# One mLSTM layer in one stage: attention of heads and memory placed between the weight steps of 25 blocks

## What is computed

```python
h = rmsnorm(x, norm_g)
qk, v, o, z, i_pre, f_pre, mq, mz = split_cols(
    h @ w_in, [2 * M_WIDTH, M_WIDTH, M_WIDTH, M_WIDTH, M_HEADS, M_HEADS, MEM_WIDTH, MEM_WIDTH])
qk = jax.nn.silu(causal_conv(qk, conv_w, conv_b))
q, k = split_cols(qk, [M_WIDTH, M_WIDTH])
ht = mlstm_chunkwise(q, k, v, i_pre + ig_b, f_pre + fg_b)      # 4 heads of 256
ht = rmsnorm(ht, h_g)
y_m = jax.nn.sigmoid(o) * ht * jax.nn.silu(z)
y_mem = memory_attention(mq, mz, mk, mv, mq_gain)              # 4 heads of 128, 256 memory slots
return x + jnp.concatenate([y_m, y_mem], axis=-1) @ w_out
```

## Time and profile before

| | |
|---|---|
| median of three runs | 2470.48 us |
| profiled execution | 2471.05 us |
| its span, first to last instruction | 2468.8 us |
| TensorE matmuls, busy | 2256.1 us (91%) |
| VectorE, busy | 1781.2 us (72%) |
| ScalarE, busy | 1412.3 us (57%) |
| mean granted clock of TensorE | 0.968 |

### The profile page before, as it was taken

The page is one execution under the profiler, slowest core; times in us unless marked ns, Lnnn a source line. Parts: engine busy times, 40 slices in busy tenths (PEclk is TensorE's granted clock), DMA queues, the critical chain, the costliest instruction groups (busy, mean ns, idle before and its releaser), DMA issues. The chain is left out here.

```text
span 2468.8 us, 31012 instructions
## 1 busy us (share of the span) xinstructions
PE 2256.1 (91%) x11018; PEld 1608.0 (65%) x11018; DVE 1781.2 (72%) x2306; ACT 1412.3 (57%) x1780; POOL 288.1 (12%) x148
## 2 busy tenths in 40 slices
PE   5998888699999999999999999499998887989989
PEld 5996665455555655555555555277786666877767
DVE  4426657688898888888889888566755665785564
ACT  3334435576777777777677777355553354665543
POOL 0008104111111011111111100000000000020000
PEclk9999899899999999999999999799998999999999
DMA  3232043599999999999999999322122001121200
GB/s 108 85 103 86 1 156 121 185 341 366 376 372 381 379 371 372 380 376 375 373 373 375 376 381 367 124 103 103 68 103 102 1 1 47 53 89 69 103 1 35
DMA packets 162760, 504.79 MB, mean 204 GB/s; under 512 B 12768, under 2 KB 28800, under 8 KB 162672
## 3 DMA queue, kind: packets, MB, share of 16 engines
q1 hardware_dynamic: 159088, 494.98, 53.6%
q0 software_dynamic: 3584, 8.66, 1.5%
HBM read 492.85 MB, written 10.75 MB: 204 GB/s over the span
## 5 line engine op out<-in xcount | busy, mean ns | idle before, releaser
L1350 DVE TENSOR_TENSOR pieces_low<-pieces,pieces_high 128x2048 fp32r<-128x2048 f32 x384 | 873.6, 2290 | 125.5 <-ACT pieces_high L1306 122.3
L1306 ACT ACTIVATE pieces_high<-pieces 128x2048 fp32r<-128x2048 f32 x384 | 732.7, 1916 | 260.5 <-PE ps L1237 260.2
L1237 PE MATMUL ps<-pieces_high,ex_x 128*66 128x512 f32 x2048 | 567.9, 394 | 5.1 <-DVE ex_hidden L1360 3.0
L1237 PEld LDWEIGHTS ps<-pieces_high,ex_x 128*66 128x66 f32 x2048 | 277.7, 137 | 193.1 <-issue 5.8
L539 DVE TENSOR_TENSOR in_w<-ring,in_w 128x512 fp32r<-128x512 f32 (+4 forms) x268 | 157.8, 589 | 241.5 <-ACT in_w L533 240.8
L1237 PE MATMUL ps<-pieces_low,ex_x 128*66 128x512 f32 x1024 | 320.0, 394 | 0.0
L1237 PE MATMUL ps<-pieces_high,ex_h 128*66 128x512 f32 x1024 | 289.2, 394 | 10.8 <-DVE pieces_low L1350 9.0
L533 ACT ACTIVATE in_w<-ring 128x512 fp32r<-128x512 f32 (+4 forms) x268 | 141.2, 528 | 265.5 <-PE ps L486 163.3
L486 PE MATMUL ps<-in_a,in_w 128*128 128x512 f32 (+1 forms) x1176 | 273.3, 393 | 7.9 <-DVE in_a L539 7.9
L486 PEld LDWEIGHTS ps<-in_a,in_w 128*128 128x128 f32 (+1 forms) x1176 | 218.3, 187 | 61.2 <-DVE in_a L539 13.6
L1237 PEld LDWEIGHTS ps<-pieces_high,ex_h 128*66 128x66 f32 x1024 | 136.9, 136 | 109.0 <-DVE pieces_low L1350 19.8
(11 more groups left out here) (376 smaller groups left out, 2522.5 us busy)
## 6 DMA issues: line engine op xcount, KB each, us to landing
pieces<-in_w_gate SPq DMA_DIRECT2D x128, 1024.0 KB, 7.3
pieces<-in_w_up SPq DMA_DIRECT2D x128, 1024.0 KB, 7.6
pieces<-in_w_down SPq DMA_DIRECT2D x128, 1024.0 KB, 9.0
ring<-in_a_w_in SPq DMA_DIRECT2D x12, 2048.0 KB, 7.5
ring<-in_w_in SPq DMA_DIRECT2D x12, 1024.0 KB, 5.0
ring<-in_mem_w_kv SPq DMA_DIRECT2D x4, 2048.0 KB, 8.7
ring<-in_b_w_in SPq DMA_DIRECT2D x4, 2048.0 KB, 7.6
ring<-in_a_w_out SPq DMA_DIRECT2D x2, 3072.0 KB, 13.9
```

Source lines behind the costliest of these rows:

```text
L1237: ins = pe.matmul(ps[0:CAP, banks + c, :], parts[a][:, k0 + k, :], w[b][:, k, c * 512:(c + 1) * 512], start=start and k == 0 and a == b == ...
L1306: nc.scalar.activation(m.high[:, n % NSPLIT, :], m.pieces[:, n % NPIECE, :], ACT.Copy).then_inc(high_done, 1)
L1350: nc.vector.tensor_tensor(m.low_part[:, n % NSPLIT, :], m.pieces[:, n % NPIECE, :], m.high[:, n % NSPLIT, :].bitcast(F32), ALU.subtract).t ...
```

## The change

The four stages of the mLSTM layer ahead of the output become one, `mixing_stage`. Its weights come as 25 blocks of at most 256 columns: gates with the first memory queries, memory queries, memory gates, q and k, v, then z and o in turns. The normed activations are split once, during the first block, and kept (`halves`, in the parts of the ring that narrow blocks leave free); all other steps split the weights alone, into 4 slots (NS). Products use three accumulators; the rest go to the attention. The gates are computed by tokens, so they need no transposes. The decays are made by tile: within a tile from the triangular mask, and from an earlier tile only up to that tile's end; the rest of the way is a number per row (`reach`) that enters as the bias of the exponential, one exponential for each tile of 128 columns. The division by the denominator moves into the norm of the head. Each head is normed and turned by itself. All work of gates, memory attention and heads is placed by step numbers between the products on each engine's queue. The scaling of the memory queries goes to GpSimd. The weights of the output projection are sent after the last product. By these formulas the steps of the first unit of each head (`begin`) are 138, 150, 162 and 174 of 200, its decays (`prepare`) 126, 142, 154 and 166, its last turning (`finish`) 161, 173, 182 and 194, and the memory units begin at steps 104 to 134.

```diff
-MLSTM_IN = [("gates", 0, 5120, 8), ("qk", 0, 0, 512), ("v", 0, 2048, 512), ("qk", 1, 512, 512), ("v", 1, 2560, 512),
-            ("qk", 2, 1024, 512), ("o", 0, 3072, 512), ("qk", 3, 1536, 512), ("o", 1, 3584, 512),
-            ("z", 0, 4096, 512), ("z", 1, 4608, 512), ("mq", 0, 5128, 512),
-            ("mz", 0, 5640, 512)]
+
+
+MIXING = ([(5120, 136), (5256, 256), (5512, 128), (5640, 256), (5896, 256)] + [(256 * i, 256) for i in range(12)]
+          + [(start + 256 * i, 256) for i in range(4) for start in (4096, 3072)])
...
-                return self.jobs[j][key][:, k]
+                return self.jobs[j][key](k)
...
-def mlstm_in_stage(m, hn, qk, v, y, mq, gates, at):
...
-def mlstm_stage(m, qk, v, gates, ht, y, at):
...
+class PackGemm(SplitGemm):
...
+    def main_units(self, j):
+        if self.jobs[j]["kind"] == "features":
+            return self.m.blocks[self.first + j][2] // P
+        return -(-4 // self.per_bank(j))
...
+    def multiply(self, pe, unit, w, a, first, last):
...
+        cols, per = self.m.blocks[self.first + unit.job][2], self.per_bank(unit.job)
+        for b in range(psum.shape[1]):
+            t0 = (per * u + b) * P
+            for i, (x, y) in enumerate(((0, 0), (0, 1), (1, 0))):
+
+                ins = pe.matmul(psum[:, b, :], a[:, x, t0:t0 + P], w[:, y, 0:cols],
+                                start=(first and i == 0 and b == 0),
+                                stop=(last and i == 2 and b == psum.shape[1] - 1))
+        return ins
...
+def mixing_stage(m, hn, qk, v, y, mq, mk, mv, at):
...
+    halves = [m.at(f"hn2_split{i}", [P, 4, 2, SEQ], m.ring_at + (3 * i + 1) * SLOT * 4, F32R) for i in range(2)]
+    kept = lambda k: halves[k // 4][:, k % 4]
...
+    def job(kind, take):
+        return dict(kind=kind, act=hn, engine="act", take=take, early=True, spread=1)
+
+    jobs = [job("tokens", take_gates), job("tokens", take_tokens(mq, P)), job("tokens", take_tokens(mq, 3 * P))]
+    jobs += [job("features", take_silu(f0)) for f0 in (8, 10)]
+    jobs += [job("features", take_qk(2 * i)) for i in range(8)]
+    jobs += [job("tokens", take_tokens(v, 256 * i)) for i in range(4)]
+    for i in range(4):
+        jobs += [job("features", take_silu(2 * i)), job("features", take_o(2 * i))]
+    MQ, MZ, QK, V, Z = 2, 3, 5, 13, 17
+    for j, x in enumerate(jobs):
+        x["split" if j else "keep"] = kept
+    work_at = m.arena + at - 24640
+    g = PackGemm(m, "in2", jobs, [work_at + 2048 * i for i in range(4)], banks=3)
...
+    begin = lambda h, t: first_step(Z) + 2 + 3 * (4 * h + t)
+    prepare = lambda h: begin(h, 0) - (8 if h else 12)
+    finish = lambda h: begin(h, 3) + (14 if h < 2 else 11)
+    opened_at = lambda n: place(Z + 1 + 2 * (n // 2), n % 2) + 1
+    asked = lambda u: first_step(Z) - 32 + 2 * u
+    gates_at = place(0, 1) + 1
+    mq_at = place(MQ) + 1
...
+            sp.wait_ge(g.used, len(g.steps))
+            g.send(sp, ahead=2)
...
+            def decays(h):
+
+                pe.wait_ge(s["built"], h + 1)
+                if h == 0:
+                    pe.wait_ge(s["mq_taken"], MEMH)
+                else:
+                    pe.wait_ge(s["exped"], 4 * h)
+                if h >= 3:
+                    pe.wait_ge(s["y_taken"], 2 * (h - 2))
+                for j in range(4):
+                    pe.matmul(ps[:, 3, j * P:(j + 1) * P], m.upto, b[:, j, :], start=True, stop=True)
+                for i in range(3):
+                    ins = pe.matmul(ps[:, 4, i * P:(i + 1) * P], m.ones, b[:, i, :], start=True, stop=True)
+                ins.then_inc(s["decayed"], 1)
...
+            def scores(u):
+                h, t = units[u]
+                if u == 0:
+                    pe.wait_ge(s["ma_pt_ready"], 16)
+                else:
+                    pe.wait_ge(s["p_ready"], u)
+                if t == 0:
+                    pe.wait_ge(s["silu_done"], NQK)
+                for k in range(2):
+                    ins = pe.matmul(ps[:, 5, 0:(t + 1) * P], qk[:, 2 * h + k, t * P:(t + 1) * P],
+                                    qk[:, 8 + 2 * h + k, 0:(t + 1) * P], start=(k == 0), stop=(k == 1))
+                ins.then_inc(s["scored"], 1)
...
+            work = {}
+            add(work, gates_at + 5, sum_gates)
+            for h in range(MEMH):
+                add(work, mq_at + 12 + h, lambda h=h: turn_mq(h))
+            for u in range(16):
+                add(work, asked(u), lambda u=u: ask(u))
+                add(work, asked(u) + 3, lambda u=u: turn_asked(u))
+                add(work, asked(u) + 5, lambda u=u: answer(u))
+            for h in range(MH):
+                add(work, prepare(h), lambda h=h: decays(h))
+                add(work, finish(h), lambda h=h: turn_h(h))
+            for u, (h, t) in enumerate(units):
+                add(work, begin(h, t), lambda u=u: scores(u))
+                add(work, begin(h, t) + 2, lambda u=u: turn(u))
+                add(work, begin(h, t) + 4, lambda u=u: values(u))
+            g.products(pe, work)
...
+            work = {}
+            add(work, gates_at + 1, gate_exp)
+            add(work, gates_at + 3, gate_log)
+            add(work, mq_at, squares_mq)
+            add(work, mq_at + 3, root_mq)
+            for h in range(MEMH):
+                add(work, mq_at + 15 + h, lambda h=h: take_mq(h))
+            for n in range(NQK):
+                add(work, place(QK + n // 2, n % 2) + 4, lambda n=n: silu(n))
+            for u in range(16):
+                add(work, asked(u) + 3, lambda u=u: ma_exp(u))
+                add(work, asked(u) + 6, lambda u=u: take_asked(u))
+            for h in range(MH):
+                for j in range(4):
+                    add(work, prepare(h) + 5 + j, lambda h=h, j=j: exps(h, j))
+                add(work, begin(h, 3) + 9, lambda h=h: root(h))
+            for u, (h, t) in enumerate(units):
+                add(work, begin(h, t) + 5, lambda u=u: take_turned(u))
+                add(work, begin(h, t) + 7, lambda u=u: take_values(u))
+            g.split("act", act, work)
...
+            work = {}
...
+            add(work, mq_at + 1, sums_mq)
+            add(work, mq_at + 4, inverse_mq)
+            for n in range(NQK):
+                add(work, place(QK + n // 2, n % 2) + 1, lambda n=n: convolve(n))
+            for u in range(16):
+                add(work, asked(u) + 3, lambda u=u: ma_max(u))
+                add(work, asked(u) + 4, lambda u=u: ma_norm(u))
+                add(work, asked(u) + 8, lambda u=u: ma_take(u))
+            for h in range(MH):
+                add(work, prepare(h), lambda h=h: build(h))
+                add(work, prepare(h) + 3, lambda h=h: maxima(h))
+                add(work, prepare(h) + 4, lambda h=h: peaks(h))
+                add(work, begin(h, 3) + 8, lambda h=h: variance(h))
+                add(work, begin(h, 3) + 9, lambda h=h: inverse(h))
+                add(work, finish(h) + 3, lambda h=h: take_h(h))
+            for n in range(MW // P):
+                add(work, opened_at(n), lambda n=n: open_gate(n))
+            for u, (h, t) in enumerate(units):
+                add(work, begin(h, t) + 3, lambda u=u: weigh(u))
+            for u, (h, t) in enumerate(units):
+                work.setdefault(begin(h, t) + 8, []).insert(0, lambda u=u: squares(u))
+            g.split("dve", dve, work)
...
+        @block.gpsimd
+        def _(pool):
+            pool.wait_ge(s["mq_inverse"], 1)
+            x = mq[:].rearrange("p t (g w) -> p t g w", g=MEMH)
+            nc.gpsimd.tensor_tensor(x, x, ms[:, 2].unsqueeze(3).to_broadcast([P, 4, MEMH, MEMD]),
+                                    ALU.mult).then_inc(s["mq_scaled"], 1)
...
-        for _, _, start, width in MLSTM_IN:
+        for start, width in MIXING:
...
-        mlstm_in_stage(m, hn, qk, v, y, mq, gates, work)
-        m.close()
-        ht = m.low("ht", [P, 4, MW], 0)
-        mlstm_stage(m, qk, v, gates, ht, y, work)
-        m.close()
-        group_norm_stage(m, "gq1", [dict(src=by_head(mq[:]), dst=mqt, gain=("mem_q", 0),
-                                         factor=MEMD ** -0.5)], work)
-        m.close()
-        attention_stage(m, "ma1", memory_units(mqt, mk[0], mv[0], y), work)
+        mixing_stage(m, hn, qk, v, y, mq, mk[0], mv[0], work)
```

More of the change, by code:

```diff
@@ L736, in projection_stage @@
     for j, job in enumerate(jobs):
-        job["split" if j else "keep"] = kept
+        job["split" if j else "keep"] = lambda k: kept[:, k]
     g = PairGemm(m, "in1", jobs, slots, banks=3)
@@ L1736, in f, with take_o @@
             return None
         return f
-    def take_v(block):
+    def take_o(n0):
         def f(step, u, psum):
[L1741 to L1753, removed]
+            n = n0 + u
@@ L1771, in mlstm_in_stage @@
[L1771 to L1792, removed]
@@ new lines, in mixing_stage, with first_step, place, taken @@
+    MQ, MZ, QK, V, Z = 2, 3, 5, 13, 17
[3 more added lines that the diff above has]
```

(52 more changed lines are left out.)

569 lines of the change are left out of this document (305 added, 264 removed).

## The result

The changed kernel takes 2456.3 us (median of 4 runs, 2454.3 to 2459.3), the kernel before 2470.5 (2469.0 to 2476.2); the ratio is 0.9939, 95% interval 0.9921 to 0.9958. It is faster by 14 us, a third of the 42.7 forecast. 2456.3 lies at the upper edge of the range, 2412 to 2457. The profiled execution took 2454.3 us, span 2452.4.

A forecast was written before the change was run, and what follows sets the result against it. TensorE was taken as the bound. 0.2 (first step) + 342.5 (TensorE's work) + 6.5 (stalls) + 12.3 (output weights) + 2.2 (low clock) = 363.7 against 406.4 us, 42.7 less, giving 2428 us; range 2412 to 2457.

The forecast's parts named there:

- Products: TensorE's product matmuls of the mLSTM input, 25 blocks in 200 steps: 273.7 us together, against 276.6 before.
- the price of the blocks of 136 and 128 columns: 192 narrow product matmuls on TensorE at 0.085 us each: 16.3 us, bounds 11.5 to 22.8.
- the 361.5 forecast for this figure: Time from the layer's first product to the output projection's first product: 406.4 us before, 361.5 forecast.
- the clock stay at 1.0 from first to last product: Sign of being right: TensorE's granted clock stays at 1.0 between first and last product, some 349 us apart.
- Attention between the steps: Head, memory and gate work put between product steps on TensorE's queue: 68.8 us, with TensorE staying the bound.
- Forecast were 349.0: Stage from first to last product: TensorE's own work of 342.5 us plus stalls of 6.5.
- Stalls: TensorE's waits within the stage: 2.0 us at convolutions, 4.0 at accumulators, 0.5 elsewhere, 6.5 together.
- At the convolutions: After each of eight qk blocks, two convolutions on VectorE delay weight splits: 0.25 us each, 2.0 together.
- the takes with a table switch: ScalarE empties accumulators late behind a table switch: eight block ends at 0.5 us, 4.0 together.
- Output weights: Load sent only after the last product: 12.3 us pause before the output's first product, then 2.2 us lost at low clock.
- go in step: Rival: a stall at every piece put between products, 100 us if nothing is hidden, so 2528 us; chance 0.08.
- ScalarE's switches weigh more: Rival: block ends lose 2 us rather than 0.5 and narrow products cost 0.119: 2445 to 2455 us; chance 0.14.

The follow-up runs named there:

- with the clock repaired: Changed kernel with its blocks of 136 and 128 columns loaded as 256 columns, only the needed ones taken: 2442.4 us, 0.9878 of the kernel before.

## Why the prediction was wrong

- **Products.** The step that failed is the price of the blocks of 136 and 128 columns, "192 matmuls ... I take 0.085 ... 16.3". At full clock those of 128 columns start every 0.1125 us (96 in 10.8, the third block of the kernel with its sums moved out, line below), which is hardly less than 256 columns (0.119): 21.6 us, 5.3 more, near the upper bound of 22.8. Worse, that term was priced at full clock. The two stretches at half clock cost 19.0 us. Together 24.3 of the 29.3 us by which 390.8 exceeds the 361.5 forecast for this figure. The prediction asked of the new profile that the clock stay at 1.0 from first to last product; that line showed it wrong at once.

```profile
L1742 PE MATMUL ps<-in_w,hn_split 128*128 128x128 f32 x96 | 10.8, 274 | 0.0
```

- **Attention between the steps** was right. Where it runs, from 1659 us, no wait of TensorE is over 1.9 us, and with the clock repaired the stage took 360.7 us. Forecast were 349.0, or 355.5 with the narrow products at 0.119, so 5 us are left. Where a piece can be read alone it costs what was counted: turning two tiles and six products of 512 columns take 1.60 us together (1845.08 to 1846.68 in the changed kernel), counted were 0.21 + 1.39. Two of the 5 us lie at the convolutions, below; the others are not settled.
- **Stalls**, 6.5 forecast. At the convolutions TensorE is idle for 1.7 us, forecast 2.0, but a block of q and k takes 11.64 us from start to start where 48 x 0.2317 = 11.12 were counted, so each block end costs 0.5 and the eight 4: the matmuls on either side of a wait start further apart too. For the takes with a table switch, 4.0 forecast, only 1.1: there are 21 table loads as counted, but most takes come behind a step that has attention in it. That this gives them time is my reading, no run shows it. At the first memory unit stand 1.9 and 0.4 that had no place in the sum. The 2.66 us for a switch that the Trainium skill states ("ScalarE: Activation LUTs", section "What `ACT_TABLE_LOAD` costs") are not seen here either: the next activation starts 1.30 us after the load does.

```profile
1700.46 11.41 PE L1734 MATMUL ps<-hn_split,in_w 128*128 128x512 f32 x48 [0.17 <-DVE in_w L539]
1712.10 11.41 PE L1734 MATMUL ps<-hn_split,in_w 128*128 128x512 f32 x48 [0.23 <-DVE in_w L539]
```

- **Output weights**: pause 12.2 us for 12.3 and 1.9 us of low clock behind it for 2.2. Right.
- **Rivals.** The queues do not go in step: TensorE's waits in the whole stage are 5 us. "ScalarE's switches weigh more" gives nearly the measured time with the wrong mechanism, and it had set the range's upper end; that 2456.3 falls just inside 2457 is luck. What happened, a low clock without a pause, stood among none of them; the low clocks of the earlier trace rows had been read as the mark of idle time only, though one of them (0.74 over the gates) holds the same small sums beside 7.5 us of idle time.

## What to carry to other kernels

A stage moved beside others takes its small matmuls with it, and they can cost more than their own microseconds: 2.3 us of them (at full clock) began a stretch at half clock that, followed by matmuls of 128 columns, cost nine. Read the granted clock beside the busy share, since a TensorE that is busy for 100% may run at half speed, and put tiny matmuls among wide ones. When a buffer is taken over for something kept until the end of a stage, the next stage's first load becomes bare: price its landing, and free first the part that is needed first.

## What was not expected of the hardware

- At full clock matmuls of 128 columns, each with a load of 128 weights, start every 0.1125 us (96 in 10.8 us, 192 in 21.6), those of 256 columns every 0.119. To compute twice the columns needed and drop half costs nearly nothing.
- A dip of the clock is short or long by what follows. After the start of the stage, the small sums or a wait of 1.9 us it lasted from none to 6.8 us where the products had 256 or 512 columns, 17 to 24 us where they had 128 or 136 (the wait never met those). Narrow products by themselves (21 us on end) did not cause one in the middle of the stage. Why the dip at the stage's first block begins, and whether the 3 us without work ahead of it are needed for that, was not tried.
